# One expert row in sixteen dotted on GpSimd and ScalarE in the gather stage of a transformer layer

## The chip, the cores and the metric

One core of a Trainium2 chip runs the whole layer as one program. The metric is the device time of one execution in microseconds (us); the lower the better. Times of several executions are given as their median.

## The reference

The layer takes 256 tokens of width 2048 in fp32: a mixer of three kinds of attention, then a product-key expert layer (PEER), then a gated per-layer embedding, then a norm. What the change touches is PEER and, at its edge, the product `p @ ple_proj`:

```python
def peer_ffn(x, wq, subkeys, u, v):
    q = (x @ wq).reshape(b, s, PEER_HEADS, 2, PEER_DQ // 2)
    sc = jnp.einsum('bshcd,hckd->bshck', q, subkeys)
    top_s, top_i = lax.top_k(sc, PEER_TOPK)
    ...
    best_s, best_j = lax.top_k(cand, PEER_TOPK)      # 16 of 16 x 16 pairs
    expert = take_along_axis(cand_i, best_j)         # 16 of 16384 rows
    g = jax.nn.softmax(best_s, axis=-1)
    def tok_fn(args):
        xc, ec, gc = args
        act = jax.nn.gelu(jnp.einsum('td,tkd->tk', xc, u[ec]), approximate=False)
        return jnp.einsum('tk,tkd->td', gc * act, v[ec])

    h = h + gate * (p[i] @ ple_proj[i])
```

For each of 256 tokens and 8 heads, 16 rows of `u` (2048 wide, 8 KB each) are gathered and dotted with the token's normed vector `xn`.

## The kernel before

Tokens lie on the 128 partitions, in two tiles of 128. The first stages (projections, attention, output projection, queries `wq`) are products on TensorE. Then comes the gather stage: 16 steps (`PEER_STEPS`), one for each tile and head; steps 0 to 7 are tile 0, steps 8 to 15 tile 1. After it the rows of `v` are weighted and summed (the dense stage, from about 1200 us), and the gate stage ends the kernel.

*One step.* GpSimd's `fetch` issues 16 indirect DMAs (k = 0 to 15, L724), each of which brings one expert row for each of the 128 tokens: 128 x 8 KB = 1.05 MB. They land in a ring of 8 buffers (`early_rows` or `late_rows`, which are names for the places of `rows` and three early ones); before the fetch of k it waits until VectorE has used the row that lay there, counted in the semaphore `eaten`. VectorE's `peer_step` waits for each row and does one instruction (L1590): the row times `xps` (a copy of `xn` in PSUM) with the sum over 2048 elements into `dots[b][:, k]`.

*The routing of the next step* is threaded in. VectorE finds the best keys and pairs of step s+1 between the dots k=0 to k=5 of step s (`best_keys` to `split_pairs`, L1506 to L1558). GpSimd turns them into expert numbers: `unpack` behind the fetch of k=13 (`PICK_AT`; it waits for VectorE's pairs, which are there after the dot k=5), `look_up` behind k=14, `name_experts` behind k=15. Only then can it fetch k=0 of step s+1. All of this is one instruction queue, in this order.

*ScalarE* does, for each step, `route_exp` (softmax of the next step's scores), `step_scores`, in steps 8 to 15 also four groups of one-hots for tile 0 with their copies out of PSUM (`tile0_hots`, `take_spread`), and then `gelu` of the 16 dots, for which VectorE waits in `coefficients`, behind the dot k=4 of the next step.

*p.* At the end of step 3 TensorE multiplies `p` with `ple_proj`; ScalarE copies the result into `pp_made` (L1111), whose place the rows of tile 1 and others need later, and from there into `pp_keep` (L1118), in the place of `xn`. SyncE (SP) writes it to memory (`ppdram`, 2 MB) after the last dot, between its loads of `vraw`; the gate stage loads it again.

*The end of the stage.* GpSimd waits for `eaten` of all steps, weighs tile 1's one-hots (L785), waits for the write of p, and fetches the rows of `v` (L770), partly into the place of `xn`.

Of the kernel before, what the change touches and what calls it, by code (L numbers as in the profile page):

```python
# [69 lines left out]
GRING = 8  # L70
SLOTS = PEER_H * TOPK
# [75 lines left out]
def build(nc, x, p, ln_mix, w_in, cmp_wk, cmp_wv, cmp_pos, out_norm, w_out, rel_bias, ln_ffn,  # L147
# [62 lines left out]
    pp_keep = at("pp_keep", 16 * KB, [P, TT, D])  # L210
# [6 lines left out]
    rows = [at(f"rows{r}", (96 + 8 * r) * KB, [P, D]) for r in range(GRING)]  # L217

# [111 lines left out]
    xt_ss, half_hi, half_lo = sem("xt_square_sums"), sem("first_halves_high"), sem("first_halves_low")  # L330
# [26 lines left out]
    r_small = sem("r_small")  # L357
# [15 lines left out]
    eaten = sem("rows_used")  # L373
    gelu_ready = sem("gelu_ready")
# [10 lines left out]
    U_FETCHES = PEER_H * TT * TOPK // GRING  # L385
# [43 lines left out]
    PEER_STEPS = TT * PEER_H  # L429
    PAIRS = PEER_STEPS // 2  # L430
# [20 lines left out]
    def products_for(g):  # L451
        return RING * (g // 2 + 1) if g // 2 < WIDE_TURNS else 2 * g + 2

# [4 lines left out]
    with block:  # L458
        @block.sync
        def _(sp):  # L460
# [9 lines left out]
            def stream(stage, ngroups, after=None, between=None):  # L470


                w = weights_of(stage)
                view = w[0].rearrange("(h k q) c -> q h k c", q=P, k=CHUNK_K)
                wide_view = w[0].rearrange("(h k q) c -> q h k c", q=P, k=CHUNK_K // 2)

                def turn(i, peeled, narrow=False):
                    for r in range(RING):

                        if not peeled:  # L480
                            sp.wait_ge(lo_ready[stage], i * RING + r - RING + 1)
                        elif after:

                            sp.wait_ge(lo_ready[after], 2 * NG[after] - RING + r + 1)
                        col = (2 * i + r // 2) * CHUNK_C
                        if stage == "gate" and not peeled:
                            sp.nop(nofuse=True)
                        if narrow:
                            sp.dma_start(raw[r][:, :, :], view[:, r % 2, :, bass.ds(col, CHUNK_C)])\
                                .then_inc(landed[r], 16)  # L490
                        else:
                            sp.dma_start(wide(raw[r]), wide_view[:, r, :, bass.ds(2 * i * CHUNK_C, 2 * CHUNK_C)])\
                                .then_inc(landed[r], 16)

                turn(0, True)
                if between:
                    between()
                if stage == "gate":
                    sp.wait_ge(clo_ready, NKEYS)
                    sp.wait_ge(pp_out, 16)  # L500
                    sp.dma_start(pp[:, :, :], ppdram).then_inc(pp_in, 16)
                for i in range(1, ngroups // 2):
                    turn(i, False, narrow=i >= WIDE_TURNS)

            for n in range(IN_CHUNKS):
                g, half, r = IN_ORDER[n // 2], n % 2, n % RING
                if n >= RING:
                    sp.wait_ge(lo_ready["in"], n - RING + 1)
# [53 lines left out]

            sp.wait_ge(routed, PEER_STEPS)
# [32 lines left out]
        def _(pool):  # L596
# [28 lines left out]
            pool.dma_start(rsmall.rearrange("o (h l) -> (o h) l", h=NH), rvec[:, :]).then_inc(r_small, 16)  # L625
            pool.wait_ge(r_small, 16)
# [11 lines left out]
            pool.wait_ge(r_out, 16)  # L638
# [69 lines left out]
            def fetch(pairs, peeled, last=False, rings=2 * [late_rows]):  # L708
                for b in range(2):
# [3 lines left out]
                    for k in range(TOPK):  # L713
                        slot = k % GRING
                        if peeled and b == 0:
                            if k >= GRING // 2:
                                pool.wait_ge(eaten, k - GRING // 2 + 1)
                        else:
                            if peeled and k < WQ_AHEAD:
                                pool.wait_ge(mm_done["wq"], WQ_RING + WQ_AHEAD)  # L720
                            pool.wait_ge(eaten, s * TOPK + k - GRING + 1)
                        pool.nop(nofuse=True)
                        dst = ring[slot]
                        pool.indirect_dma_start(dst[:, :], None, peer_u[0],  # L724
                                                bass.IndirectOffsetOnAxis(ap=expert[b][:, k:k + 1], axis=0))\
                            .then_inc(fetched[slot], 16)
                        if b == 0 or not last:
# [4 lines left out]
                            if k == PICK_AT + 2:  # L732
                                name_experts(s + 1, 1 - b)

# [13 lines left out]
            fetch(PAIRS - 1, False, last=True)  # L748
# [27 lines left out]
            pool.wait_ge(eaten, PEER_STEPS * TOPK)  # L776
# [19 lines left out]
            pool.wait_ge(pp_out, 16)  # L796
# [17 lines left out]
        def _(act):  # L814
# [6 lines left out]
            def half_high(c):  # L821
# [5 lines left out]
                act.copy(whi[n % 2][:, ks, :], raw[n][:, ks, :]).then_inc(hi_ready["in"] if h else half_hi, 1)  # L827
# [39 lines left out]
            act.copy(zsum[0][:, 0:1], ones[:, 0:1])  # L867
# [182 lines left out]
            def gelu(turn, b):  # L1050
                act.wait_ge(eaten, (2 * turn + b + 1) * TOPK)
# [65 lines left out]
            for tt in range(TT):  # L1117
                act.copy(pp_keep[:, tt, :], pp_made[:, tt, :]).then_inc(pp_sb, 1)  # L1118
# [27 lines left out]
            def peer(i, spreading, last, first=False):  # L1146
                for b in range(2):
# [12 lines left out]
                    gelu(i, b)  # L1160
# [6 lines left out]
            act.wait_ge(pp_sb, 8 + TT)  # L1167
# [13 lines left out]
            def v_halves(i, r, peeled=False):  # L1181

                c = VBODY * i + r
                if peeled and r == 0:
                    act.wait_ge(pp_out, 16)
# [80 lines left out]
        def _(dve):  # L1266
# [15 lines left out]
            def half_low(c):  # L1282
                n, h = divmod(c, 2)
                dve.wait_ge(hi_ready["in"] if h else half_hi, n + 1)
                ks = slice(h * XK, (h + 1) * XK)
                dve.tensor_tensor(wlo[n % 2][:, ks, :], raw[n][:, ks, :], whi[n % 2][:, ks, :].bitcast(fp32), ALU.subtract)\
                    .then_inc(lo_ready["in"] if h else half_lo, 1)
# [51 lines left out]
            def in_lo(n):  # L1339
                dve.wait_ge(hi_ready["in"], n + 1)  # L1340
# [242 lines left out]
            def peer_step(turn, b, tt, first=False, last=False, ring=late_rows):  # L1583

                s = 2 * turn + b
                for k in range(TOPK):

                    dve.wait_ge(fetched[k % GRING], (s * (TOPK // GRING) + k // GRING + 1) * 16)
# [85 lines left out]
            dve.wait_ge(eaten, PEER_STEPS * TOPK)  # L1674
# [11 lines left out]
            def use_v_row(i, r, tt, peeled):  # L1686

                n = TT * r + tt
                dve.wait_ge(fetched[n % VROWS], 16 * (U_FETCHES + TT * VBODY // VROWS * i + n // VROWS + 1))
# [117 lines left out]
        def _(pe):  # L1807
# [59 lines left out]
            def in_chunk(j):  # L1867
# [3 lines left out]
                if j < HALVED:  # L1871
                    pe.wait_ge(half_lo, j + 1)
                else:
                    pe.wait_ge(lo_ready["in"], j + 1)
                if half == 0 and n >= 3:
                    pe.wait_ge(evac["in"], n - 1)
                for k in range(CHUNK_K):
# [3 lines left out]
                    if j < HALVED and k == XK:  # L1881
                        pe.wait_ge(lo_ready["in"], j + 1)
# [435 lines left out]
```

## Time and profile before

| what | before |
|---|---|
| median of 3 executions | 1796.42 us (1790.77 to 1802.18) |
| the profiled execution, span from first to last instruction | 1792.3 us |
| TensorE's mean granted clock | 0.840 of 2.4 GHz |
| DMA, mean over the span | 321 GB/s, 575.07 MB |

The profile is of one execution, whose own span is 1792.3 us. A busy time is the sum over an engine's instructions, whatever they lay beside; a stage is therefore read from the stretch in which it runs. In the order of time, each line has the start, the duration, the engine, the line of the kernel, the operation and what it writes from what; in brackets stands how long the engine had been idle and what ended that. L1590 is a row's dot on VectorE, L724 a row's fetch on GpSimd (the duration is that of issuing it, not of the transfer).

### The profile page before, as it was taken

To read this page: it belongs to the slowest core of one execution; us is meant where nothing else is said; L and a number is where in the kernel's file an instruction comes from. 1 tells how busy PE (TensorE), PEld (TensorE's weight loads), DVE (VectorE), ACT (ScalarE), POOL (GpSimd) and SP (SyncE) were. 2 spreads that over 40 slices of the span, in tenths; PEclk is the share of its full clock that TensorE was granted. 3 is DMA by queue.
4 is the path that set the end of the run, shared out by engine and by line. 5 is a ranking of instruction groups with operands and counts; after the bars stand their busy time and mean duration, and the time that the engine had idled before them with its cause. 6 is when DMAs were issued, how large, how long until landed. Compare 5 with 4: busy or idle time off the path is not lost. (4 is left out here: it accounts for less than half of the span.)

```text
span 1792.3 us, 23540 instructions
## 1 busy us (share of the span) xinstructions
PE 1272.3 (71%) x7451; PEld 1152.3 (64%) x7451; DVE 1469.4 (82%) x1998; ACT 784.9 (44%) x1353; POOL 814.4 (45%) x824
## 2 busy tenths in 40 slices
PE   9999999999992450000221221399999999999997
PEld 8999999989982430000111111378998899999887
DVE  6435556764679999999999999889999999999855
ACT  6324445544211130011666666574444444444644
POOL 1200000000154555555555555288888887887303
PEclk9999999999996785555555555599999999999999
DMA  9964444367899999999999999829999999999953
GB/s 299 314 204 152 142 142 142 120 233 265 325 384 422 412 412 410 404 406 418 414 402 399 410 409 412 371 71 377 373 354 357 365 370 374 367 375 375 344 189 117
DMA packets 157735, 575.07 MB, mean 321 GB/s; under 512 B 14597, under 2 KB 72278, under 8 KB 121697
## 3 DMA queue, kind: packets, MB, share of 16 engines
q0 software_dynamic: 58544, 362.96, 50.9%
q1 hardware_dynamic: 99120, 211.20, 33.8%
q8 instruction: 41, 0.67, 0.2%
q14 instruction: 30, 0.24, 0.0%
HBM read 569.89 MB, written 7.36 MB: 322 GB/s over the span
## 5 line engine op out<-in xcount | busy, mean ns | idle before, releaser
L1590 DVE SCALAR_TENSOR_TENSOR rows<-rows,banks 128x2048 f32<-128x2048 f32 x214 | 480.2, 2280 | 20.0 <-DMA rows<-peer_u_dram,expert 19.8
L724 POOL DMA_INDIRECT rows<-peer_u_dram,expert x214 | 204.2, 954 | 398.4 <-DVE expert L1627 154.7
L770 POOL DMA_INDIRECT vrow<-peer_v_gathered_dram,vidx x224 | 334.5, 1493 | 80.4 <-DVE hres L1692 42.4
L2198 PE MATMUL banks<-hot,hot 128*128 128x128 f32 x512 | 103.3, 368 | 237.1 <-ACT hot L1143 233.2
L2198 PEld LDWEIGHTS banks<-hot,hot 128*128 128x128 f32 x512 | 89.3, 264 | 251.5 <-issue 178.2
L834 ACT CAST whi<-raw 128x2048 fp32r<-128x2048 f32 x77 | 146.7, 1905 | 228.1 <-PE banks L1894 145.1
L1692 DVE SCALAR_TENSOR_TENSOR hres<-vrow,slot_coef,hres 128x672 f32<-128x672 f32 x224 | 204.6, 913 | 12.0 <-DMA vrow<-peer_v_gathered_dram,vidx 11.9
L1706 DVE TENSOR_TENSOR vlo<-vraw,vhi 128x1376 fp32r<-128x1376 f32 x128 | 202.8, 1584 | 4.5 <-ACT vhi L1193 3.9
L2225 PE MATMUL banks<-vhi,chi 128*128 128x460 f32 x762 | 181.4, 373 | 3.0 <-ACT vhi L1193 3.0
L2232 PE MATMUL banks<-vlo,chi 128*128 128x460 f32 x762 | 179.6, 370 | 3.5 <-DVE vlo L1706 3.4
L2225 PE MATMUL banks<-vhi,clo 128*128 128x460 f32 x762 | 179.8, 371 | 0.0
L1193 ACT CAST vhi<-vraw 128x1376 fp32r<-128x1376 f32 x128 | 172.1, 1345 | 7.5 <-DMA vraw<-peer_v_dense_dram 7.0
L1188 ACT CAST chi<-spread 128x256 fp32r (+1 forms) x128 | 52.1, 407 | 261.9 <-PE banks L2232 261.9
L1341 DVE TENSOR_TENSOR wlo<-raw,whi 128x2048 fp32r<-128x2048 f32 x45 | 103.4, 2298 | 70.9 <-ACT whi L834 68.4
L1894 PE MATMUL banks<-xthi,whi 128*128 128x256 f32 x544 | 156.6, 288 | 1.9 <-DVE xtlo L1278 1.7
L2232 PEld LDWEIGHTS banks<-vlo,chi 128*128 128x128 f32 x762 | 143.2, 188 | 20.7 <-DVE vlo L1706 5.5
L2225 PEld LDWEIGHTS banks<-vhi,chi 128*128 128x128 f32 x762 | 144.2, 189 | 18.9 <-issue 3.1
L2225 PEld LDWEIGHTS banks<-vhi,clo 128*128 128x128 f32 x762 | 144.3, 189 | 15.2
L1894 PE MATMUL banks<-xthi,wlo 128*128 128x256 f32 x544 | 153.9, 283 | 0.0
L1894 PE MATMUL banks<-xtlo,whi 128*128 128x256 f32 x544 | 153.9, 283 | 0.0
L2183 PE MATMUL banks<-ident,slot_idx 128*128 128x128 f32 x4 | 1.4, 449 | 192.0 <-DVE slot_coef L1579 192.0
L2183 PEld LDWEIGHTS banks<-ident,slot_idx 128*128 128x128 f32 x4 | 0.6, 204 | 193.1 <-DVE slot_coef L1579 193.1
(299 smaller groups left out, 2946.0 us busy)
## 6 DMA issues: line engine op xcount, KB each, us to landing
vraw<-peer_v_dense_dram SPq DMA_DIRECT2D x128, 688.0 KB, 7.4
raw<-w_in_dram SPq DMA_DIRECT2D x45, 1024.0 KB, 5.5
raw<-w_out_dram SPq DMA_DIRECT2D x16, 1024.0 KB, 5.3
raw<-ple_gate_dram SPq DMA_DIRECT2D x16, 1024.0 KB, 5.5
wqraw<-peer_wq_packed_dram SPq DMA_DIRECT2D x12, 1024.0 KB, 8.7
wq_ahead<-peer_wq_packed_dram SPq DMA_DIRECT2D x4, 1024.0 KB, 8.0
vrow<-peer_v_gathered_dram,vidx POOLq DMA_INDIRECT x224, 7.5
rows<-peer_u_dram,expert POOLq DMA_INDIRECT x214, 12.4
```

The lines of the kernel that those rows point to most:

```text
L724: pool.indirect_dma_start(dst[:, :], None, peer_u[0], bass.IndirectOffsetOnAxis(ap=expert[b][:, k:k + 1], axis=0))\
L770: pool.indirect_dma_start(vrow[j][:, :], None, v_gathered, bass.IndirectOffsetOnAxis(ap=idx[:, j % TT, j // TT:j // TT + 1], axis=0))\
L834: act.copy(whi[r % 2][:, :, :], raw[r][:, :, :]).then_inc(hi_ready[stage], 1)
L1193: act.copy(vhi[r % 2][:, :], vraw[r % VRING][:, :]).then_inc(vhi_ready, 1)
L1341: dve.tensor_tensor(wlo[n % 2][:, :, :], raw[n % RING][:, :, :], whi[n % 2][:, :, :].bitcast(fp32), ALU.subtract).then_inc(lo_ready["in"], 1)
L1590: dve.scalar_tensor_tensor(out=r[:, :], in0=r[:, :], scalar=1.0, in1=xps[tt][:, :], op0=ALU.mult, op1=ALU.mult, accum_out=dots[b][:, k:k + ...
L1692: dve.scalar_tensor_tensor(out=hres[:, tt, 0:VGATH], in0=vrow[n % VROWS][:, :], scalar=slot_coef[:, bass.ds(VBODY * i + r + tt * SLOTS, 1) ...
L1706: dve.tensor_tensor(vlo[r % VRING][:, :], vraw[r % VRING][:, :], vhi[r % 2][:, :].bitcast(fp32), ALU.subtract).then_inc(vlo_ready, 1)
L1894: last = pe.matmul(acc[:, u * SEQ:(u + 1) * SEQ], a, b, start=half == 0 and k == 0 and u == 0 and m == 0, stop=half == 1 and k == CHUNK_K ...
L2198: last = pe.matmul(bank[SPREAD_BANK[m]][:, a * P:(a + 1) * P], hot2[tt][m][:, a, :], hot1[tt][m][:, a, :], start=True, stop=True)
L2225: last = pe.matmul(dst, x[:, tt, :], vhi[r % 2][:, cols], start=first and x is chi[0], stop=False, skip_group_check=True)
L2232: last = pe.matmul(dst, chi[r % 2][:, tt, :], vlo[r % VRING][:, cols], start=False, stop=False, skip_group_check=True)
```

## The change

From step 4 on (`SIDE_FROM`), the row k=8 (`SIDE`) of each step is fetched into a buffer of its own (`rows[7]` in steps 4 to 7, `side_row` in steps 8 to 15), by a DMA that stands behind the fetch of k=6 and waits until ScalarE has summed the side row of the step before. GpSimd multiplies it in place by `xn`, in an instruction that stands at the very end of the step's part of its queue: behind `name_experts`, ahead of the next step's k=0. ScalarE sums the products into `dots[b][:, 8]` (a copy with an accumulated output), ahead of `gelu`. VectorE skips k=8, so the ring has 15 rows a step. The counts that stood for 16 rows a step change accordingly (`dots_through`, `slot_free`, `U_FETCHES`).

`xn` must now last until the last product, so `pp_keep` goes: SyncE writes `pp_made` to memory as soon as it is whole, in step 4. GpSimd waits for the end of the query products before step 4 (was: before step 8), and before step 8 for the last product of p and for step 7's sum. To free semaphores, three pairs of them are merged in the first stage and in the bias table, with the counts rewritten (`in_split`); these edits are left out below.

```diff
@@ fetch, GpSimd @@
+            def side_fetch(s, b, row):
+                pool.wait_ge(side_dotted, s - SIDE_FROM + 1)
+                pool.nop(nofuse=True)
+                pool.indirect_dma_start(row[:, :], None, peer_u[0],
+                                        bass.IndirectOffsetOnAxis(ap=expert[b][:, SIDE:SIDE + 1], axis=0))\
+                    .then_inc(side_landed, 16)
+
+            def side_products(s, row, tt):
+                pool.wait_ge(side_landed, 16 * (s - SIDE_FROM + 1))
+                pool.nop(nofuse=True)
+                pool.tensor_tensor(row[:, :], row[:, :], xn[:, tt, :], ALU.mult).then_inc(side_made, 1)
...
                     for k in range(TOPK):
+                        if side is None or k != SIDE:
...
+                            elif side is not None:
+                                pool.wait_ge(eaten, slot_free(s, k))
...
+                        if side is not None and k == 6:
+                            side_fetch(s, b, side)
                         if b == 0 or not last:
                             if k == PICK_AT:
                                 unpack(s + 1)
...
                             if k == PICK_AT + 2:
                                 name_experts(s + 1, 1 - b)
+                    if side is not None:
+                        side_products(s, side, tt)
...
+            pool.wait_ge(mm_done["wq"], WQ_PER * NG["wq"])
             with pool.Fori(2, HALF) as i:
-                fetch(i, False, rings=2 * [early_rows])
+                fetch(i, False, rings=2 * [early_rows], side=rows[7], tt=0)
...
-            pool.wait_ge(mm_done["wq"], WQ_PER * NG["wq"])
+            pool.wait_ge(side_dotted, 2 * HALF - SIDE_FROM + 1)
+            pool.wait_ge(pp_mm, 8)
             with pool.Fori(HALF, PAIRS - 1) as i:
-                fetch(i, False)
+                fetch(i, False, side=side_row, tt=1)
...
-            pool.wait_ge(pp_out, 16)
+            pool.wait_ge(side_made, PEER_STEPS - SIDE_FROM)
@@ ScalarE @@
+            def side_dot(s, b, row):
+                act.wait_ge(side_made, s - SIDE_FROM + 1)
+                act.activation(row[:, :], row[:, :], ACT.Copy, accum_out=dots[b][:, SIDE:SIDE + 1]).then_inc(side_dotted, 1)
+
+            def gelu(turn, b, side=None):
+                s = 2 * turn + b
+                if side is not None:
+                    side_dot(s, b, side)
+                    act.wait_ge(side_dotted, s - SIDE_FROM + 2)
+                act.wait_ge(eaten, dots_through(s + 1))
...
-            for tt in range(TT):
-                act.copy(pp_keep[:, tt, :], pp_made[:, tt, :]).then_inc(pp_sb, 1)
@@ peer_step, VectorE @@
                 for k in range(TOPK):
+                    if side and k == SIDE:
+                        continue
@@ SyncE @@
             sp.dma_start(ptile[:, :, :], p[0, 0].rearrange("(t q) c -> q t c", q=P)).then_inc(p_in, 16)
 
+            sp.wait_ge(pp_sb, 8)
+            sp.dma_start(ppdram, pp_made[:, :, :]).then_inc(pp_out, 16)
...
-                if c == VRING - 1:
-                    sp.wait_ge(pp_sb, 8 + TT)
-                    sp.wait_ge(eaten, PEER_STEPS * TOPK)
-                    sp.dma_start(ppdram, pp_keep[:, :, :]).then_inc(pp_out, 16)
```

## Rows read from the trace of the kernel before

**Rows 1.** The page, busy times over the whole span: us, share, instructions

```profile
PE 1272.3 (71%) x7451; PEld 1152.3 (64%) x7451; DVE 1469.4 (82%) x1998; ACT 784.9 (44%) x1353; POOL 814.4 (45%) x824
```

**Rows 2.** A stretch of the gather stage: PE, PEld, DVE, ACT, POOL, PEclk, DMA share, GB/s

```profile
760.00:820.00 60.00, 0.00 (x0) 0.00 (x0) 59.46 (x80) 7.14 (x13) 34.40 (x50) 0.50 1.01 410
```

**Rows 3.** Order of time: k=5; k=15, k=0 issued; k=15, 0, 1, 5; k=0 issued

```profile
759.79 2.27 DVE L1590 SCALAR_TENSOR_TENSOR rows<-rows,banks 128x2048 f32<-128x2048 f32 x1
...
771.10 0.99 POOL L724 DMA_INDIRECT rows<-peer_u_dram,expert  x1 [0.90 <-DVE early_rows L1590]
...
776.70 1.03 POOL L724 DMA_INDIRECT early_rows<-peer_u_dram,expert  x1 [0.92 <-POOL slot_row L702]
...
782.01 2.28 DVE L1590 SCALAR_TENSOR_TENSOR rows<-rows,banks 128x2048 f32<-128x2048 f32 x1
...
784.22 2.28 DVE L1590 SCALAR_TENSOR_TENSOR early_rows<-early_rows,banks 128x2048 f32<-128x2048 f32 x1
...
786.83 2.27 DVE L1590 SCALAR_TENSOR_TENSOR early_rows<-early_rows,banks 128x2048 f32<-128x2048 f32 x1
...
800.90 2.27 DVE L1590 SCALAR_TENSOR_TENSOR rows<-rows,banks 128x2048 f32<-128x2048 f32 x1
...
818.09 1.03 POOL L724 DMA_INDIRECT rows<-peer_u_dram,expert  x1 [1.22 <-issue]
```

**Rows 4.** Order of time in step 15: dots k=0, 11, 12, 15, and the vraw loads

```profile
1113.05 2.28 DVE L1590 SCALAR_TENSOR_TENSOR rows<-rows,banks 128x2048 f32<-128x2048 f32 x1
...
1142.13 2.29 DVE L1590 SCALAR_TENSOR_TENSOR rows<-rows,banks 128x2048 f32<-128x2048 f32 x1 [0.19 <-DMA rows<-peer_u_dram,expert]
1143.32 1.75 SPq L569 DMA_DIRECT2D vraw<-peer_v_dense_dram  x4
...
1144.61 2.29 DVE L1590 SCALAR_TENSOR_TENSOR rows<-rows,banks 128x2048 f32<-128x2048 f32 x1 [0.19 <-DMA rows<-peer_u_dram,expert]
...
1151.26 2.29 DVE L1590 SCALAR_TENSOR_TENSOR rows<-rows,banks 128x2048 f32<-128x2048 f32 x1 [1.87 <-DMA rows<-peer_u_dram,expert]
```

**Rows 5.** GpSimd's groups by shape: count, busy us, mean ns, idle before

```profile
L785 POOL TENSOR_TENSOR hot<-hot,tsl 128x512 f32<-128x512 f32 x32 | 33.3, 1042 | 27.7 <-DVE hot L1569 23.7 <-issue 3.9
...
L810 POOL TENSOR_TENSOR xn<-hres,gain 128x512 f32<-128x512 f32 x7 | 15.9, 2293 | 73.6 <-DMA gain<-ln_final_dram 70.9 <-DVE hres L1743 2.7
...
L620 POOL TENSOR_TENSOR wlo<-raw,whi 128x2048 fp32r<-128x2048 f32 x1 | 4.6, 4603 | 12.4 <-ACT whi L834 12.4
...
L652 POOL TENSOR_TENSOR pr<-pr 128x768 f32<-128x768 f32 x1 | 1.8, 1842 | 204.3 <-ACT pr L925 204.3
```

**Rows 6.** From issue to use: landing of L724, 640 to 860; first rows, steps 0, 1

```profile
DMA to landing us min/median/max: 5.4/12.4/16.9
...
472.85 1.05 POOL L724 DMA_INDIRECT rows<-peer_u_dram,expert  x1 [154.74 <-DVE expert L1627]
...
478.62 2.29 DVE L1590 SCALAR_TENSOR_TENSOR rows<-rows,banks 128x2048 f32<-128x2048 f32 x1 [6.51 <-DMA rows<-peer_u_dram,expert]
...
524.11 1.03 POOL L724 DMA_INDIRECT early_rows<-peer_u_dram,expert  x1 [0.93 <-POOL slot_row L702]
...
530.70 2.29 DVE L1590 SCALAR_TENSOR_TENSOR early_rows<-early_rows,banks 128x2048 f32<-128x2048 f32 x1 [3.73 <-DMA early_rows<-peer_u_dram,expert]
...
535.35 2.29 DVE L1590 SCALAR_TENSOR_TENSOR early_rows<-early_rows,banks 128x2048 f32<-128x2048 f32 x1 [1.96 <-DMA early_rows<-peer_u_dram,expert]
```

**Rows 7.** Two short stretches: while GpSimd issues every 1.25 us, and later

```profile
781.00:787.00 6.00, 0.00 (x0) 0.00 (x0) 6.00 (x9) 0.22 (x1) 4.64 (x5) 0.50 0.97 345
...
790.00:796.00 6.00, 0.00 (x0) 0.00 (x0) 5.72 (x12) 0.00 (x0) 1.75 (x2) 0.50 1.02 429
```

**Rows 8.** Order of time, ScalarE in step 4

```profile
665.74 3.70 ACT L1118 COPY pp_keep<-pp_made 128x2048 f32<-128x2048 f32 x2
```

**Rows 9.** Order of time, ScalarE in step 9: behind T, and the last copy

```profile
885.62 0.20 ACT L1030 ACTIVATE nbest<-best 128x1 f32<-128x1 f32 x1 [12.94 <-DVE bidx L1558]
...
911.14 1.04 ACT L1123 COPY spread<-banks 128x512 f32<-128x512 f32 x1 [1.21 <-PE banks L2198]
```

More of the change, by code:

```diff
@@ L429, in build, with dots_through, slot_free @@
     PEER_STEPS = TT * PEER_H
+    def dots_through(s):
+        return (SIDE_FROM * TOPK + (TOPK - 1) * (s - SIDE_FROM)) if not isinstance(s, int) or s >= SIDE_FROM else s * TOPK
+    def slot_free(s, k):
+        return (TOPK - 1) * (s - SIDE_FROM) + SIDE_FROM * TOPK - GRING + k + 1
     PAIRS = PEER_STEPS // 2
@@ L452, in products_for, with in_split @@
         return RING * (g // 2 + 1) if g // 2 < WIDE_TURNS else 2 * g + 2
+    def in_split(n):
+        return 2 * n if n < HALVED else n + HALVED
     def weights_of(stage):
@@ L482, in turn @@
                         elif after:
-                            sp.wait_ge(lo_ready[after], 2 * NG[after] - RING + r + 1)
+                            sp.wait_ge(lo_ready[after], in_split(2 * NG[after] - RING + r + 1))
                         col = (2 * i + r // 2) * CHUNK_C
@@ L706, in _, with fetch @@
             PICK_STEPS = 11
-            def fetch(pairs, peeled, last=False, rings=2 * [late_rows]):
+            def side_fetch(s, b, row):
[8 more added lines that the diff above has]
+                pool.tensor_tensor(row[:, :], row[:, :], xn[:, tt, :], ALU.mult).then_inc(side_made, 1)
+            def fetch(pairs, peeled, last=False, rings=2 * [late_rows], side=None, tt=0):
                 for b in range(2):
@@ L826, in half_high @@
                 ks = slice(h * XK, (h + 1) * XK)
-                act.copy(whi[n % 2][:, ks, :], raw[n][:, ks, :]).then_inc(hi_ready["in"] if h else half_hi, 1)
+                act.copy(whi[n % 2][:, ks, :], raw[n][:, ks, :]).then_inc(hi_ready["in"], 1)
             def split_hi(stage, turn, r, peeled):
@@ L866, in _ @@
             act.wait_ge(const_ready, 1)
-            act.copy(zsum[0][:, 0:1], ones[:, 0:1])
+            act.copy(zsum[0][:, 0:1], ones[:, 0:1]).then_inc(side_dotted, 1)
             act.wait_ge(gain_in, 16)
@@ L1159, in peer @@
                         take_spread(0, q + PER_STEP - 1, PER_STEP - 1)
-                    gelu(i, b)
+                    gelu(i, b, side=side_row if spreading else rows[7])
             with act.Fori(2, HALF) as i:
@@ L1283, in half_low @@
                 n, h = divmod(c, 2)
-                dve.wait_ge(hi_ready["in"] if h else half_hi, n + 1)
+                dve.wait_ge(hi_ready["in"], c + 1)
                 ks = slice(h * XK, (h + 1) * XK)
                 dve.tensor_tensor(wlo[n % 2][:, ks, :], raw[n][:, ks, :], whi[n % 2][:, ks, :].bitcast(fp32), ALU.subtract)\
-                    .then_inc(lo_ready["in"] if h else half_lo, 1)
+                    .then_inc(lo_ready["in"], 1)
             dve.wait_ge(gain_in, 16)
@@ L1585, in peer_step @@
                 s = 2 * turn + b
+                side = not isinstance(s, int) or s >= SIDE_FROM
                 for k in range(TOPK):
-                    dve.wait_ge(fetched[k % GRING], (s * (TOPK // GRING) + k // GRING + 1) * 16)
+                    if side and k == SIDE:
+                        continue
+                    before = s + SIDE_FROM if side and k % GRING == SIDE % GRING else s * (TOPK // GRING) + k // GRING
+                    dve.wait_ge(fetched[k % GRING], (before + 1) * 16)
                     r = ring[k % GRING]
```

64 lines of the change are left out of this document (31 added, 33 removed).

## Prediction

> **What bounds the kernel now.** I read four views, from coarse to fine. The page [rows 1] gives VectorE (DVE) the largest busy share, but an average over stages says little. The table of stretches [rows 2] does: from 760 to 820 us VectorE is busy 59.46 of 60 us, the DMA engines are busy too (share 1.01, 410 GB/s) and TensorE idles at a granted clock of 0.50. This is the gather stage, 16 steps of 16 expert rows, and every step that the change touches (4 to 15) lies in it.
>
> The order of time of one step [rows 3] shows who sets its length. Let T be the end of the dot k=5 (759.79 + 2.27 = 762.06, next 803.17). The period is 41.1 us, and VectorE has no gap before any row dot: it is the bound. A plain dot repeats every 2.21 us; from the start of k=0 (784.22) to the end of k=5 (803.17) it takes 18.9 us, since the routing of the next step is threaded between those dots.
>
> GpSimd (POOL) runs a chain anchored at T: it issues k=13, then works through its three routing parts with k=14 and k=15 between them (k=15 at 771.10, T+9.0), and issues k=0 of the next step at 776.70 (T+14.6; T+14.9 at the next boundary, 818.09; I use 14.8). VectorE reaches k=0 at 784.22, T+22.2. So the next step's first row is issued only 7.2 to 7.5 us before it is wanted (784.22 + 41.11 = 825.33 for the second), and that margin is what the change spends.
>
> How near the DMA engines are to being the bound is seen in step 15, which has no routing [rows 4]: rows arrive 2.48 us apart and VectorE waits for each a little. Sixteen rows so cost 39.7 us, 1.4 us below the present period. With one dot fewer VectorE alone would need 41.1 - 2.2 = 38.9 us, so 39.7 is the floor, whatever else is arranged. By the Trainium skill ("DMA: Bandwidth & Descriptors", Where 436 GB/s comes from) the port ceiling is 435 GB/s; as an estimate, 16.78 MB would take 38.6 us. The measured 2.48 us a row decides here, and is a little slower.
>
> **The change, part by part.** *The dot that goes.* In steps 4 to 15 VectorE skips k=8: 2.21 us a step, 26.5 us in all, if nothing else ends later. The row still comes from memory, so the DMA saves nothing.
>
> *The product on GpSimd.* Its place decides: at the end of a step's fetches, behind the naming of the next experts and ahead of the fetch of k=0. It is a 128x2048 multiply in place. Nearest rows [rows 5]: a subtraction of the same shape, 4.60 us (L620); the in-place add L652 of 768 elements, 1.84 us, which scales to 4.9 for 2048; four times the 512-element L785, 4.2 us. I take L620's 4.6, between the two, lower bound 4.2. L810 costs 2.29 us for 512 elements, which would make 9.2; it stands in the last stage, beside other work of VectorE. By the Trainium skill ("GPSIMD Engine Reference", Key points) GpSimd contends with VectorE instructions that have two SBUF inputs; here VectorE runs only row dots just then (one input in SBUF, one in PSUM). By that rule the price stays 4.6; no run here shows GpSimd at this product beside them.
>
> A wait with a computing instruction behind it costs some 0.2 us on this queue. The issue of k=0 moves from T+14.8 to T+14.8+4.6+0.2 = T+19.6. The side row itself is no delay: it is issued behind k=6, some 25 us before its product.
>
> *What is late next: k=0.* VectorE, now a dot shorter, wants it at T+20.0. From issue to landing takes at least 5.4 us, and the stage's very first fetch was used 5.77 us after issue (472.85 to 478.62) [rows 6]. Queued rows don't lengthen this: the last issue before k=0 is k=15, at T+9.0. From the former k=0, the other fifteen transfers at 2.48 us bring k=15 about T+18.3. I take 5.6, lower bound 5.5 to the use. Upper bound: step 1's first row, 6.59 us (524.11 to 530.70) with weights still streaming.
>
> So k=0 starts at T+25.2, and k=5 ends 18.9 us later. Right after a slow patch of GpSimd, while it issues every 1.25 us, the DMA moves just 345 GB/s (3.0 us a row) against 429 later [rows 7]; k=1 is wanted 2.6 us behind k=0, so add 0.3 (lower 0, upper 2.0, from the 4.65 us between the first two rows of step 1 [rows 6]). New period: 19.6 + 5.6 + 18.9 + 0.3 = 44.4 us, 3.3 above 41.1. The dots k=6 to k=15 end sooner than this and only wait: the saved 2.2 us sits inside a new hole of some 5 us ahead of k=0. From step 4's T to step 15's T there are 11 periods: +36.3 us.
>
> *Step 15 from k=0 on.* Before 40.4 us (1113.1 to 1153.5). Now 16 rows in a row from k=0's landing: 15 x 2.48 + 2.2 = 39.4, plus about 2 for the slow start, plus the four vraw loads, which already held up the last row by 1.9 us [rows 4] and now meet about one row more (1.5): 42.9, so +2.5 (from -0.5 to +4).
>
> *ScalarE (ACT).* Its sum over 2048 elements is like a copy of that size, 1.85 us (two in 3.70) [rows 8]. In steps 4 to 7 it ends before T+21.6, while GpSimd needs the buffer again behind k=6, at T+28. In steps 8 to 14 it stands behind the tile-0 one-hots, whose last copy ends about T+26.8 (T just before 885.6, the copy's end 912.2) [rows 9], so the buffer is free at T+28.8 against GpSimd's T+28.4: nothing, as k=0 to k=6 are queued by then. Without that cover each further us would reach k=7 only. The exception is the new wait before step 8, which needs step 7's sum before k=0: 1.9 + 0.2, +2.1 once.
>
> *p goes out at once.* The two copies into pp_keep (3.70 us of ScalarE at 665.7 [rows 8]) are followed by nothing that VectorE waits for before the next routing: 0. The 2 MB write moves from the end of the stage to shortly before those copies' time, into step 4's dots k=0 to k=5. At 410 GB/s it is 5.1 us of DMA work, which rows ahead of their use mostly absorb: +1 (0 to 5). At its old place, behind the last dot, it lay beside the making of tile 1's one-hots and delayed nobody: 0. The merged semaphores of the first stage wait for the same events as before: 0; the wait for the query products ahead of step 4 is met, since those products end before step 3's dots do: 0.
>
> Sum: 36.3 + 2.5 + 2.1 + 1.0 = +41.9 us. The profiled execution's span was 1792.3 us, 4.1 below the median of 1796.4; with the same 4.1 around it, 1792.3 + 41.9 + 4.1 = **1838 us**.
>
> **Rivals.** (a) *The margin holds, the dot saved is a gain* (faster than before). The mechanism is the flight time of k=0: if it lands by T+20.8, the DMA's 39.7 us period rules. Gain 11 x 1.4 = 15.4 us, less 2.1 + 1 + 0.5 for the single places: 1785 us, still within 1% of before. For it: GpSimd has gaps elsewhere and the DMA never stops. Against: GpSimd's product and the flight would together have to fit into 20.8 - 14.8 - 0.2 = 5.8 us, where the rows say 10.2; even equality with before (k=0 at T+22.2) asks for 7.2. By the ceiling of 435 GB/s of the Trainium skill (the same page and section) VectorE's 38.9 would rule instead, and the estimate would be 1776 us. At the 429 GB/s that the DMA reaches for a while [rows 7], the period would be 39.1 us and the time 1778 us, just over 1% faster. Chance of all this 6%, of the last 2%.
> (b) *Margin half spent*: product 4.2, flight 5.5, no stall at k=1: 43.3 us a period, +24 and +2 to +3 around it: about 1823 us. A still shorter pair, 8 us, gives some 1807. Together 16%, half of it inside 1%.
> (c) *Slow product*: GpSimd and VectorE block each other as L810's rate allows. 9.2 us instead of 4.6: 49.0 a period, +87 us, 1889 us. Against: the dots keep 2.27 to 2.28 us whether GpSimd routes beside them or not [rows 3]. 7%.
> (d) *Cold DMA*: flight 6.6 and 2.0 at k=1, as in step 1: 47.1 a period, +66 and up to 10: about 1870 us. Step 1 had the weights beside it, which steps 4 on have not. 11%.
>
> **Chances and range.** Forecast (44.0 to 45.5 a period) 60%, (a) 6%, (b) 16%, (c) 7%, (d) 11%. A measurement of this kernel tells about 1% (18 us) from no change. Slower by over 1%: 60 + 8 + 7 + 11 = 86; within 1%: 4 + 8 = 12; faster: 2. The range holds the forecast, the upper part of (b) and the lower part of (d): 1815 to 1862 us.
>
> **What would show it.** In the changed profile: ahead of every k=0 dot of steps 5 to 15 a VectorE gap of 4 to 6 us ended by the row's DMA, and hardly any gap elsewhere; the product's row near 4.6 us, x12; k=0 issued at T+19.6; the period 44 to 45 us in steps 4 to 14, still 41.1 before; the rate of the DMA down from 410 to about 378 GB/s in the stage; the spans of the dense stage behind it unchanged, only later. Wrong is the forecast if k=0 is used within 3 us of issue, if the product runs beside the naming of experts, or if its duration is far from 4.6.

## The result and the profile after

| | before | after |
|---|---|---|
| median of 6 executions | 1791.66 us | 1835.76 us (1832.80 to 1843.91) |
| ratio to before, 95% interval | | 1.0233 (1.0208 to 1.0259) |
| span of the profiled execution | 1792.3 us | 1835.5 us |

The change makes the kernel 2.3% slower. The busy times of the page (answering [rows 1]) hide it: VectorE does less than before, and waits.

```profile
PE 1275.2 (69%) x7451; PEld 1155.9 (63%) x7451; DVE 1452.8 (79%) x1974; ACT 802.8 (44%) x1375; POOL 862.4 (47%) x836
```

The table of stretches of the changed kernel, 700 to 1100 us (columns as in [rows 2]), shows where: VectorE is busy 352 of 400 us, the DMA engines' share is 0.93 and they move 379 GB/s. In the kernel before the same stretch has 394.64 us, 1.00 and 409 GB/s (second fence).

```profile
700.00:1100.00 400.00, 46.56 (x180) 39.73 (x180) 352.35 (x534) 180.96 (x426) 240.50 (x280) 0.50 0.93 379
```

```profile
700.00:1100.00 400.00, 52.64 (x203) 45.02 (x203) 394.64 (x601) 180.69 (x451) 214.39 (x287) 0.50 1.00 409
```

The order of time around the boundary from step 8 to step 9 in the changed kernel answers [rows 3]. L1636 is a dot, L756 a ring fetch, L735 the product, L727 the side fetch, L1091 the sum on ScalarE.

```profile
859.20 2.27 DVE L1636 SCALAR_TENSOR_TENSOR rows<-rows,banks 128x2048 f32<-128x2048 f32 x1
...
870.53 0.99 POOL L756 DMA_INDIRECT rows<-peer_u_dram,expert  x1 [0.90 <-DVE rows L1636]
...
875.01 0.20 POOL L717 CAST slot_row<-bidxf 128x16 f32 x1
...
875.50 4.55 POOL L735 TENSOR_TENSOR side_row<-side_row,xn 128x2048 f32<-128x2048 f32 x1 [0.28 <-POOL slot_row L717]
877.90 2.29 DVE L1636 SCALAR_TENSOR_TENSOR rows<-rows,banks 128x2048 f32<-128x2048 f32 x1 [0.19 <-DMA rows<-peer_u_dram,expert]
880.20 1.03 POOL L756 DMA_INDIRECT rows<-peer_u_dram,expert  x1 [0.16 <-DVE rows L1636]
880.33 2.29 DVE L1636 SCALAR_TENSOR_TENSOR rows<-rows,banks 128x2048 f32<-128x2048 f32 x1
...
885.81 2.29 DVE L1636 SCALAR_TENSOR_TENSOR rows<-rows,banks 128x2048 f32<-128x2048 f32 x1 [3.18 <-DMA rows<-peer_u_dram,expert]
...
889.21 2.29 DVE L1636 SCALAR_TENSOR_TENSOR rows<-rows,banks 128x2048 f32<-128x2048 f32 x1 [0.71 <-DMA rows<-peer_u_dram,expert]
```

Read it from T, the end of the dot k=5 (859.20 + 2.27 = 861.47). GpSimd is through with the naming at 875.2, multiplies from 875.50 to 880.05, and issues k=0 at 880.20, T+18.7. VectorE ends its last dot at 882.6 and stands until 885.81: the row needs 5.61 us from issue to use. k=1 follows 3.40 us behind, where it used to follow 2.61. The time of one step, k=0 to k=0, is 44.6 us here and 44.2 us as the mean of the next five (885.81 to 1106.72), against 41.1.

### The profile page after: what moved, and what is told of

The parts are those of the page before. It is cut to its first block and busy times, and to the rows that moved or that the text cites. A ratio compares the mean times of both kernels' runs of the same rounds, so it can differ in the third digit from the quotient of the medians.

```text
span 1835.5 us, 23638 instructions
## 1 busy us (share of the span) xinstructions
PE 1275.2 (69%) x7451; PEld 1155.9 (63%) x7451; DVE 1452.8 (79%) x1974; ACT 802.8 (44%) x1375; POOL 862.4 (47%) x836
## 5 line engine op out<-in xcount | busy, mean ns | idle before, releaser
L1636 DVE SCALAR_TENSOR_TENSOR rows<-rows,banks 128x2048 f32<-128x2048 f32 x206 | 466.6, 2282 | 68.9 <-DMA rows<-peer_u_dram,expert 68.0
L756 POOL DMA_INDIRECT rows<-peer_u_dram,expert x206 | 196.6, 954 | 375.3 <-DVE expert L1673 154.7
L808 POOL DMA_INDIRECT vrow<-peer_v_gathered_dram,vidx x224 | 317.4, 1417 | 93.2 <-DVE hres L1738 47.1
L1738 DVE SCALAR_TENSOR_TENSOR hres<-vrow,slot_coef,hres 128x672 f32<-128x672 f32 x224 | 204.6, 913 | 11.1 <-DMA vrow<-peer_v_gathered_dram,vidx 10.2
L2271 PEld LDWEIGHTS banks<-vhi,chi 128*128 128x128 f32 x762 | 143.5, 188 | 18.7 <-issue 3.1
L2271 PEld LDWEIGHTS banks<-vhi,clo 128*128 128x128 f32 x762 | 144.4, 190 | 15.2
```

What stands on the lines that cost most here:

```text
L756: pool.indirect_dma_start(dst[:, :], None, peer_u[0], bass.IndirectOffsetOnAxis(ap=expert[b][:, k:k + 1], axis=0))\
L808: pool.indirect_dma_start(vrow[j][:, :], None, v_gathered, bass.IndirectOffsetOnAxis(ap=idx[:, j % TT, j // TT:j // TT + 1], axis=0))\
L1636: dve.scalar_tensor_tensor(out=r[:, :], in0=r[:, :], scalar=1.0, in1=xps[tt][:, :], op0=ALU.mult, op1=ALU.mult, accum_out=dots[b][:, k:k + ...
L1738: dve.scalar_tensor_tensor(out=hres[:, tt, 0:VGATH], in0=vrow[n % VROWS][:, :], scalar=slot_coef[:, bass.ds(VBODY * i + r + tt * SLOTS, 1) ...
L2271: last = pe.matmul(dst, x[:, tt, :], vhi[r % 2][:, cols], start=first and x is chi[0], stop=False, skip_group_check=True)
```

## Experiments

Eight kernels were run. e1 to e4 shared one chip and its runs of the kernel before (1794.97 us), e5 to e8 another (1792.82 us). The period is the mean of the six from k=0 of step 8 to k=0 of step 14 in each order of time; by the same reading it is 41.12 us in the kernel before and 44.25 us in the changed one.

| | median us | ratio to before (95%) | period |
|---|---|---|---|
| e1, half the product | 1812.08 | 1.0097 (1.0060 to 1.0134) | 41.70 |
| e2, almost no product | 1795.20 | 1.0002 (0.9978 to 1.0025) | 40.66 |
| e3, product behind k=7 of the next step | 1788.74 | 0.9973 (0.9954 to 0.9992) | 40.22 |
| e4, before plus a product in steps 8 to 14 | 1824.89 | 1.0158 (1.0115 to 1.0201) | 45.05 |
| e5, as e4, no wait behind the product | 1818.50 | 1.0138 (1.0112 to 1.0163) | 43.99 |
| e6, before plus the early write of p | 1795.88 | 1.0030 (1.0013 to 1.0048) | 41.12 |
| e7, as e3, p's write at the old place | 1783.62 | 0.9952 (0.9934 to 0.9970) | 40.33 |
| e8, as e3, one dot cut short | 1788.64 | 0.9974 (0.9957 to 0.9991) | 40.43 |

### e1: half the product

```diff
-                pool.tensor_tensor(row[:, :], row[:, :], xn[:, tt, :], ALU.mult).then_inc(side_made, 1)
+                pool.tensor_tensor(row[:, 0:D // 2], row[:, 0:D // 2], xn[:, tt, 0:D // 2], ALU.mult).then_inc(side_made, 1)
```

> GpSimd multiplies only the first half (1024 elements) of each side row by xn; the second half of that dot is summed without the product, so this dot is left wrong. Everything else is as in the changed kernel. Theory (flight): the period of a step is T to the issue of k=0, plus the row's flight of 5.6 us, plus 18.9 us; GpSimd's product lies in the first term in full. By the rows of 768 elements (1.84 us) and of 2048 (4.54 us in the changed kernel) 1024 elements take some 2.4 us, so the period falls by 2.1 us to about 42.1 and the time by 11 x 2.1 = 23 us, to about 1813 us. Rival (supply): the changed kernel is held by the DMA, whose rows arrive 2.48 us apart and for which VectorE waits at k=13 to k=15; then a shorter product changes nothing: 1836 us.

1812.08 us. The groups of GpSimd in e1 give the halved product 2.36 us instead of 4.55:

```profile
L735 POOL TENSOR_TENSOR side_row<-side_row,xn 128x1024 f32<-128x1024 f32 x8 | 18.9, 2361 | 2.0 <-POOL slot_row L717 1.9
```

The kernel takes 23.7 us less than the changed one (24 us by the ratios), 2.2 us for each of 11 boundaries: the whole of what the product lost. It lies on the path in full, and the DMA was not the bound of the changed kernel.

### e2: almost no product

```diff
-                pool.tensor_tensor(row[:, :], row[:, :], xn[:, tt, :], ALU.mult).then_inc(side_made, 1)
+                pool.tensor_tensor(row[:, 0:16], row[:, 0:16], xn[:, tt, 0:16], ALU.mult).then_inc(side_made, 1)
```

> GpSimd multiplies only the first 16 elements of each side row; the rest of that dot is left without the product. Theory (flight): the product all but goes (about 0.2 us), k=0 is used at about T+20.6, the period falls to 39.7 to 40.0 us, which is also what 16 rows cost the DMA at 2.48 us; 11 x 4.3 = 47 us less than the changed kernel, about 1789 us, so about the time of the kernel before. Rival (supply): 1836 us, or at best the 41.1 us period of before, 1802 us, if GpSimd's queue with its side fetch and waits is what costs.

1795.20 us, 6 us above what the theory expected, and no different from the kernel before. The period is 40.5 us (mean of the five from step 9 to step 14: 871.79 to 1074.07 in its order of time, so 40.46), not 39.7 to 40.0. In steps 9 to 14 VectorE waits only 0.2 to 1.2 us ahead of k=0, which is issued at T+14.8 to T+15.2 and used 5.9 to 7.1 us later, and k=1 is used up to 3.4 us behind it. How much of the 40.5 us is the rows' flight and how much the DMA's rate, e2 does not separate; e7 and e8 take this up. Two single costs stand beside it: k=0 of step 5 starts at 706.31 instead of 701.96 (the write of p), and the period into step 8 is 42.7 us (the wait for step 7's sum).

### e3: the product behind k=7 of the next step

```diff
-                        if side is not None and k == 6:
-                            side_fetch(s, b, side)
+                        if side is not None and k == 7 and (b == 1 or before):
+                            side_products(s - 1, side, tt if b == 1 or before_tt is None else before_tt)
+                        if side is not None and k == 12:
+                            if b == 0 and not before:
+                                pool.wait_ge(pp_mm, 8)
+                            side_fetch(s, b, side)
...
-                    if side is not None:
-                        side_products(s, side, tt)
+                if last:
+                    side_products(s, side, tt)
```

> All of the change, with GpSimd's product moved behind the fetch of k=7 of the NEXT step (for step 15 behind its own fetches), and the side row's fetch moved behind k=12 of its step; one buffer in all steps, so the wait before step 8 goes. Nothing is left out of the computation. Theory (flight): the product no longer stands between the naming of experts and the fetch of k=0, and lies in the time in which GpSimd waits for free buffers; k=0 is used at T+20.4, the DMA's 39.7 us rule: 11 x 1.4 = 15 us below the kernel before, plus about 2 for the early write and 2 for step 15: about 1780 us. Rival (load): the product costs GpSimd's queue its 4.5 us wherever it stands, the following rows are late instead: 1836 us. Rival (no gain from VectorE): 1792 us.

1788.74 us: 47 us below the changed kernel, with the same work on each engine (some 3 us of it because the wait before step 8 is gone as well). The order of time of e3, GpSimd alone:

```profile
899.69 1.02 POOL L756 DMA_INDIRECT rows<-peer_u_dram,expert  x1 [1.09 <-issue]
...
908.48 0.94 POOL L756 DMA_INDIRECT rows<-peer_u_dram,expert  x1 [0.30 <-issue]
909.43 4.54 POOL L735 TENSOR_TENSOR side_row<-side_row,xn 128x2048 f32<-128x2048 f32 x1
914.14 0.97 POOL L756 DMA_INDIRECT rows<-peer_u_dram,expert  x1 [0.16 <-issue]
915.50 0.94 POOL L756 DMA_INDIRECT rows<-peer_u_dram,expert  x1 [0.39 <-issue]
919.15 0.93 POOL L756 DMA_INDIRECT rows<-peer_u_dram,expert  x1 [2.72 <-DVE rows L1640]
```

The product costs its 4.54 us here too, but eight rows of the step have been issued while VectorE is only at the second (k=1 starts at 908.61), and two fetches later GpSimd waits for a free buffer again (2.72 us before 919.15). So the price of the product in the changed kernel is the price of its place. The gain over the kernel before is 0.3%, 6 us (1 to 8), where the theory expected 15: the time lies nearer to the second rival, "no gain from VectorE" (1792), than to the theory's 1780. What is missing is the early write of p (e6: some 4 us, not 2) and a floor that is 0.5 us a step higher than assumed (below).

### e4 and e5: the product without the saved dot

```diff
                                 name_experts(s + 1, 1 - b)
+                    if extra and not (last and b == 1):
+                        pool.nop(nofuse=True)
+                        pool.tensor_tensor(scratch[:, :], pp_keep[:, 0, :], pp_keep[:, 1, :], ALU.mult).then_inc(extra_made, 1)
+                        pool.wait_ge(extra_made, s - 2 * HALF + 1)
+                        pool.nop(nofuse=True)
```

> The kernel before, with all 16 dots on VectorE and the old fetches, and a GpSimd product of the same size (two constant operands into a scratch buffer, its result unused) at the place of the product, behind the naming of experts, in steps 8 to 14 only: 7 periods. Nothing is left out. Theory (flight): the period is T to issue, 14.8 + 4.5 + 0.5, plus 5.6, plus 18.9 = 44.3 us, just as in the changed kernel that has one dot fewer: 7 x 3.2 = +22 us, about 1814 us. That would show that the saved dot is worth nothing in the changed kernel. Rival (sum): the dot was worth its 2.2 us beneath the new wait, so without the saving each period is 46.4: 7 x 5.3 = +37 us, 1829 us.

e4 gave 1824.89 us, 30 us over the kernel before and between the two expectations, so it decided nothing by itself. Its order of time shows a flaw in the experiment: behind the product the fetch of k=0 starts only after 0.83 to 1.34 us (mean 1.02 over the seven; 1.34 in the rows below), against 0.16 in the changed kernel. The second wait is what differs, and e5 takes it out.

```profile
902.53 4.55 POOL L738 TENSOR_TENSOR scratch<-pp_keep 128x2048 f32<-128x2048 f32 x1 [0.21 <-POOL slot_row L704]
908.42 1.03 POOL L726 DMA_INDIRECT rows<-peer_u_dram,expert  x1 [1.34 <-issue]
```

In e5 the product's end is waited for by the users of its buffer, after the last step:

```diff
-                        pool.wait_ge(extra_made, s - 2 * HALF + 1)
-                        pool.nop(nofuse=True)
```

> As e4 (the kernel before, 16 dots on VectorE, a scratch product at the product's place in steps 8 to 14), but without the wait for that product between it and the fetch of k=0; in e4 that fetch started 1.34 us after the product's end, in the changed kernel 0.16 us. Nothing is left out. Theory (flight, the dot saved is worth nothing): T to issue is then 18.8 us as in the changed kernel, the period 18.8 + 5.6 + 19.7 = 44.1 to 44.2 us, 7 x 3.0 = +21 us against the kernel before, about 1816 us. Rival (the dot was worth something): the period stays near the 45.1 us of e4, about 1824 us, or goes to 46.4 us, 1831 us, if it was worth all of its 2.2.

```profile
902.48 4.55 POOL L738 TENSOR_TENSOR scratch<-pp_keep 128x2048 f32<-128x2048 f32 x1 [0.21 <-POOL slot_row L704]
907.18 1.03 POOL L726 DMA_INDIRECT rows<-peer_u_dram,expert  x1
```

1818.50 us. From step 8 to step 14, k=0 to k=0, e5 with 16 dots on VectorE takes 43.99 us a step (825.39 to 1089.31), the changed kernel with 15 takes 44.25 (841.22 to 1106.72). With the product in that place, the saved dot is worth nothing. Of the 1.06 us between a period of e4 and one of e5, 0.85 are the later issue of k=0 (T+19.54 against T+18.69, means of steps 9 to 14): that delay is passed on whole, and the rest is not told apart from the scatter of the rows' flight. The time is 25.7 us over the kernel before, not the 21 of the theory, since step 15 takes 44.6 us here (1132.75 to 1177.35) against 40.5.

### e6: the early write of p alone

```diff
+            sp.wait_ge(pp_sb, 8)
+            sp.dma_start(ppdram, pp_made[:, :, :]).then_inc(pp_out, 16)
+
             sp.wait_ge(routed, PEER_STEPS)
...
-            for tt in range(TT):
-                act.copy(pp_keep[:, tt, :], pp_made[:, tt, :]).then_inc(pp_sb, 1)
```

> The kernel before with the part on p alone: pp_made is written to memory as soon as it is whole, in step 4, and the copies into pp_keep are gone; all 16 dots on VectorE. Nothing is left out. Theory (absorbed): the 5.1 us of DMA work delay dots of step 4 by about 2 us, as in the changed kernel's step 4, and since VectorE is the bound after that, nothing is given back: +2 us (0 to 3). Rival (full price): all 5.1 us are paid. Second rival: the freed copies and the freed end of the stage give it back, 0 or less.

The ratio is 1.0030, 5 us (2 to 9), and the profiled execution says 3.8: its last dot ends at 1157.3 instead of 1153.6. The rival of the full price is nearer than the theory. The order of time of VectorE in e6, step 4 and the start of step 5:

```profile
673.24 2.29 DVE L1585 SCALAR_TENSOR_TENSOR rows<-rows,banks 128x2048 f32<-128x2048 f32 x1 [2.19 <-DMA rows<-peer_u_dram,expert]
...
693.65 2.29 DVE L1585 SCALAR_TENSOR_TENSOR rows<-rows,banks 128x2048 f32<-128x2048 f32 x1 [0.18 <-DMA rows<-peer_u_dram,expert]
...
706.06 2.29 DVE L1585 SCALAR_TENSOR_TENSOR early_rows<-early_rows,banks 128x2048 f32<-128x2048 f32 x1 [0.18 <-DMA early_rows<-peer_u_dram,expert]
```

The write delays k=3 by 2.2 us; then the dots from k=11 on follow the rows at 2.48 us instead of 2.21, and k=0 of step 5 starts at 706.06 instead of 701.96. Of the 5.1 us that the 2 MB should take, 4.1 are paid there, in two places: the lead of the rows was too short to hide them.

### e7 and e8: what bounds the moved product

e7 is e3 with the write at its old place (of other data), e8 is e3 with a dot that is almost left out:

```diff
# e7
-            sp.wait_ge(pp_sb, 8)
-            sp.dma_start(ppdram, pp_made[:, :, :]).then_inc(pp_out, 16)
...
+                if c == VRING - 1:
+                    sp.wait_ge(eaten, dots_through(PEER_STEPS))
+                    sp.dma_start(ppdram, xn[:, :, :]).then_inc(pp_out, 16)
# e8
-                    dve.scalar_tensor_tensor(out=r[:, :], in0=r[:, :], scalar=1.0, in1=xps[tt][:, :], op0=ALU.mult,
+                    w = 256 if side and k == 12 else D
+                    dve.scalar_tensor_tensor(out=r[:, 0:w], in0=r[:, 0:w], scalar=1.0, in1=xps[tt][:, 0:w], op0=ALU.mult,
```

> As e3 (product behind k=7 of the next step), but the 2 MB write is made at its old place, after the last dot, and from the place of xn, so that the gate stage gets other data than p's projection: the part on p is left wrong. The same bytes move. In e3 k=0 of step 5 started 3 us later than in the kernel before. Theory (the DMA is the bound in e3): work added to the DMA anywhere in the stage costs its full 5.1 us; without it the time falls by 4 to 5 us, to about 1784 us. Rival (absorbed as in e6): it falls by 2 us or less.

> As e3, but from step 4 on VectorE's dot of k=12 covers only the first 256 of 2048 elements, so this dot is left wrong; all transfers stay. VectorE then has some 1.9 us less to do in each step. Theory (the DMA is the bound in e3, at 417 GB/s and a period of 40.2 us): no change, 1789 us, and VectorE waits longer for rows. Rival (VectorE with its routing is still the bound in part): up to 12 x 1.9 = 22 us less, 1767 us.

e7 is 5.1 us below e3 (1783.62 against 1788.74, on two chips; by the ratios 0.21% or 3.8 us, and their intervals overlap). The profiled executions are clearer: k=0 of step 5 starts at 699.64 in e7 and at 704.99 in e3, and the last dot ends at 1143.23 against 1147.41. The write costs about what its bytes cost, as it did in e6 too, so e7 does not tell by itself what bounds e3. e8 is where e3 is, 1788.64 us, though VectorE has 18 us less to do between 700 and 1100 us. The first fence is the stretch in e3, the second in e8:

```profile
700.00:1100.00 400.00, 54.28 (x210) 46.58 (x211) 385.61 (x588) 206.22 (x482) 264.36 (x305) 0.50 1.01 417
```

```profile
700.00:1100.00 400.00, 53.37 (x206) 45.67 (x207) 367.52 (x590) 205.23 (x479) 263.93 (x303) 0.50 1.01 416
```

The groups of VectorE in the same stretch, first e3, then e8, show where the 18 us went: waiting for rows rose from 8.1 to 29.8 us.

```profile
L1640 DVE SCALAR_TENSOR_TENSOR rows<-rows,banks 128x2048 f32<-128x2048 f32 x134 | 302.5, 2282 | 8.1 <-DMA rows<-peer_u_dram,expert 6.3 <-issue 1.1
```

```profile
L1641 DVE SCALAR_TENSOR_TENSOR rows<-rows,banks 128x2048 f32<-128x2048 f32 x125 | 282.7, 2280 | 29.8 <-DMA rows<-peer_u_dram,expert 29.8
```

So VectorE's dots behind T no longer set the period. That the DMA does, e8 alone does not show: its short dot k=12 stands between T and the next k=0, where a saving would vanish under the chain of GpSimd and the flight as well. The order of time of e3 speaks for the DMA. It has the issue of k=14 and k=15 of step 9 and of k=0 of step 10, and the start of their dots:

```profile
890.85 1.04 POOL L756 DMA_INDIRECT rows<-peer_u_dram,expert  x1 [0.84 <-POOL pick L694]
894.03 0.99 POOL L756 DMA_INDIRECT rows<-peer_u_dram,expert  x1 [0.83 <-POOL pick L699]
899.69 1.02 POOL L756 DMA_INDIRECT rows<-peer_u_dram,expert  x1 [1.09 <-issue]
901.08 2.29 DVE L1640 SCALAR_TENSOR_TENSOR rows<-rows,banks 128x2048 f32<-128x2048 f32 x1 [0.20 <-DMA rows<-peer_u_dram,expert]
903.53 2.29 DVE L1640 SCALAR_TENSOR_TENSOR rows<-rows,banks 128x2048 f32<-128x2048 f32 x1 [0.15 <-DMA rows<-peer_u_dram,expert]
906.00 2.29 DVE L1640 SCALAR_TENSOR_TENSOR rows<-rows,banks 128x2048 f32<-128x2048 f32 x1 [0.17 <-issue]
```

The three are used some 2.5 us apart. k=14 and k=15 were issued 10.2 and 9.5 us before their use, far more than the 5.5 to 6.2 us of a row's flight, so they were held up behind other rows. k=0 takes 6.3 us and comes right behind k=15. But GpSimd's chain is close behind: with an issue at T+14.6 and a flight of 5.5 to 6.2 us, k=0 could be there at T+20.1 to T+20.8 at the earliest, and it is used at T+20.9 to T+21.4 in steps 6 to 14. A step of 16.78 MB in 40.2 us is 417 GB/s; this is the period said in other words and no second proof. From here, work taken off VectorE behind T brings nothing (e8); whether work taken off the routing between k=0 and k=5 would, no run tested.

## Why the prediction was right, step by step

**The mechanism.** All three parts held: GpSimd's chain from T sets the issue of k=0 (e1, e3, e4 against e5), the row's flight is added to it, and the saved dot is worth nothing under it (e5). The forecast, 1838 us, lies 2 us above the median of 1835.76. That it is so near is in part luck. It was an increase of 41.9 us over a median of 1796.42; the six executions of the kernel before have 1791.66, and the increase came out at 44.1 us (43.2 between the two profiled executions). Of these 43.2, 39.7 had arisen when the last dot ended, and 3.5 behind it, where nothing was forecast.

**The terms of a period** moved against each other. With boundary 8 to 9 as the example:

| term | predicted | measured | |
|---|---|---|---|
| T to the issue of k=0 | 19.6 | 18.7 | 0.9 too much |
| of this the product | 4.6 | 4.53 to 4.56, x12 | right |
| flight, issue to use | 5.6 | 5.61 | right (5.5 to 6.2 over the steps) |
| k=0 to the end of k=5, with k=1's stall | 19.2 | 19.8 | 0.6 too little |
| period | 44.4 | 44.2 (mean of steps 9 to 14) | |

The first term was too long because the gap of 0.9 us between the naming and the fetch of k=0, which stands in [rows 3], was kept and the product added to it. That gap is not a fixed cost: behind the 4.55 us product it shrank to 0.16, and in e4, with a wait in between, it is 0.83 to 1.34 again. A likely reading is that something of the fetch is prepared beside the product; no run shows what. The third was too short because k=1 is used mostly 3.1 to 3.9 us behind k=0 (2.8 in step 6, 2.6 in step 14), not 2.9. A likely reason is that the rows of the burst now start with none on their way and go at the slow rate of [rows 7]; no run isolates it.

**The sum over the stage.** From k=0 of step 4 to k=0 of step 15 the profiled execution needs 489.2 us (660.43 to 1149.58) against 452.2: +36.9, where 36.3 + 2.1 + 1.0 = 39.4 were predicted. In it, the wait before step 8 cost 2.8 us (46.98 us a period against 44.2) instead of 2.1. Its rows, in the order of time of the changed kernel:

```profile
828.11 4.53 POOL L735 TENSOR_TENSOR rows<-rows,xn 128x2048 f32<-128x2048 f32 x1 [0.29 <-POOL slot_row L717]
835.72 1.03 POOL L756 DMA_INDIRECT rows<-peer_u_dram,expert  x1 [3.08 <-DVE rows L1636]
...
841.22 2.29 DVE L1636 SCALAR_TENSOR_TENSOR rows<-rows,banks 128x2048 f32<-128x2048 f32 x1 [6.44 <-DMA rows<-peer_u_dram,expert]
```

(The releaser named there had long been done; what GpSimd waited for is ScalarE's sum, which runs from 832.67 to 834.67. The fetch then starts 1.05 us later, a gap that was put at 0.2.) Of the idle 6.44 us before k=0 of step 8, 2.8 are this wait.

**The write of p** was the term that was mis-sized: +1 was taken from a range of 0 to 5. Alone it costs 3.8 us in e6. In the changed kernel the delay of step 4's k=5 is 1.9 us (T at 681.3 where 679.8 was, from a start 0.4 us earlier); the second part, late rows behind k=5, falls into the hole ahead of k=0 there and costs nothing more. So "rows ahead of their use mostly absorb it" was wrong, and the number was near for another reason.

**Step 15.** +3.1 us (1149.58 to 1193.22, 43.6 us, against 1113.05 to 1153.55, 40.5 us), 2.5 predicted. The vraw loads met two rows instead of one, as these rows of the changed kernel show against [rows 4]:

```profile
1179.79 69.09 SPq L588 DMA_DIRECT2D vraw<-peer_v_dense_dram  x6
...
1186.80 2.29 DVE L1636 SCALAR_TENSOR_TENSOR rows<-rows,banks 128x2048 f32<-128x2048 f32 x1 [1.44 <-DMA rows<-peer_u_dram,expert]
1190.93 2.29 DVE L1636 SCALAR_TENSOR_TENSOR rows<-rows,banks 128x2048 f32<-128x2048 f32 x1 [1.84 <-DMA rows<-peer_u_dram,expert]
```

**The signs named beforehand.** The gap ahead of k=0 was said to be 4 to 6 us; it is 2.9 to 4.0 (0.4 before step 5, 6.4 before step 8). One reason is that k=0 is issued 0.9 us earlier than forecast. The other is in the sentence "hardly any gap elsewhere": the last rows come 2.48 us apart, VectorE waits some 0.2 us each for k=14 and k=15 (in step 8 from k=12 on), and it is through at T+20.7 to T+21.3, not T+20.0 (ahead of k=0 of steps 6 to 15). So part of the saved dot is lost before the big gap. The DMA rate of 378 GB/s came out at 379. "The dense stage unchanged" holds only roughly: from the last dot to the end the changed kernel's profiled execution takes 642.3 us, that of the kernel before 638.8. This stretch scatters without any tie to the gather stage (1822.7 - 1185.6 = 637.1 in e4, 1808.6 - 1166.2 = 642.4 in e1), so 3.5 of the 43 us between the two profiled executions are put down to it. That was not tested further.

**ScalarE's sum** was said to free the side buffer 0.4 us late in steps 8 to 14, at no cost. The sum ends as forecast (in step 9 at 890.15, T+28.7), but GpSimd is there at T+27.2, not T+28.4, so its side fetch starts 2.1 to 2.2 us after the fetch before it in each of steps 9 to 14, where 0.30 is usual. This is the row of step 9 in the changed kernel:

```profile
890.92 0.94 POOL L727 DMA_INDIRECT side_row<-peer_u_dram,expert  x1 [2.22 <-ACT side_row L1091]
```

Three fetches later, at 896.12, GpSimd waits 1.77 us for a free buffer again, and VectorE has no gap before k=7 to k=11 in steps 9 to 14. So the wait costs nothing, as forecast, though it is longer than forecast.

**A sum that was wrong.** Rival (b) does not add up: 14.8 + 0.2 + 4.2 + 5.5 + 18.9 is 43.6 us a period, not 43.3, and its time some 1826 us, not 1823.

**The floor.** Rival (a) put the DMA's floor at 39.7 us from step 15's rows alone. The measured period without the product in the chain is 40.2 to 40.4 (e3, e8): while GpSimd issues its burst after the naming, the DMA runs slower, 378 GB/s in e3 between 900 and 906 us against 425 in the next six:

```profile
900.00:906.00 6.00, 2.07 (x8) 1.78 (x8) 5.47 (x6) 5.97 (x17) 4.47 (x6) 0.50 0.99 378
906.00:912.00 6.00, 2.07 (x8) 1.78 (x8) 5.94 (x14) 4.46 (x9) 5.38 (x4) 0.50 1.02 425
```

With 40.2 as the floor, rival (a) would have gained 10 us over the 11 periods instead of 15. Whether the slow start comes from the burst of issues or from the few rows under way is open. The DMA share is 0.99 in it, so the engines count as busy.

**Contention of GpSimd and VectorE.** Rival (c) is out: beside the product the dots take 2.29 us, and the product 4.55 us, less than the 4.60 us of [rows 5]. The Trainium skill ("GPSIMD Engine Reference", Key points) names VectorE instructions with two SBUF inputs or in a two-port mode as those that contend with GpSimd. The trace agrees: the dots have one input in PSUM.

## What to carry to other kernels

An engine that also issues transfers has two schedules: its own work, and how long before use each transfer leaves. Work put on it costs nothing where it would wait for a free buffer and costs its full length where the next fetch is the first of a series, so the place in the queue was worth most of 47 us here, and the work itself nothing that the traces show. Before moving work off the busiest engine, look for the second bound (here 40.2 us a step against 41.1, by the rows' spacing the DMA): it caps what even the right place can bring, 0.3%.

## What the runs showed of the hardware beyond what was expected

- The 0.9 us after which a fetch on GpSimd starts behind small instructions [rows 3] is not additive: it is 0.16 us behind a 4.55 us product (changed kernel, e3, e5), but 0.83 to 1.34 us when GpSimd waits for that product's own semaphore in between (e4).
- A product's length on GpSimd is close to linear: 0.22 us for 16 elements, 2.36 for 1024, 4.55 for 2048, so some 0.2 us and 2.13 ns an element.
- Where VectorE waits for k=0 with no earlier row on its way, the row is used 5.5 to 6.2 us after its issue (changed kernel, steps 6 to 15; e1, steps 6 to 15; e4 and e5, steps 9 to 15); 1.05 MB at 417 GB/s are only 2.5 of them.
- A busy share near 1 does not say that the DMA is the bound: in the stretch from 700 to 1100 us it is 1.00 at 409 GB/s in the kernel before, where VectorE never waits for a row, and 1.01 at 417 GB/s in e3, where it does.
